# Modulation beside a feed-forward block: products on ScalarE and sums on GpSimd in place of VectorE, two steps later

## What is computed

```python
def squared_relu_mlp(h, w_up, w_down):
    return jnp.square(jax.nn.relu(h @ w_up)) @ w_down

# first block, its second half
x = x + squared_relu_mlp(rms_norm(x, norm_mlp[i]), mlp_w_up[i], mlp_w_down[i])
...
# second block: six modulation vectors for x, and for the context
mx = [m[:, None, :] for m in jnp.split(jax.nn.silu(c) @ w_mod[l] + b_mod[l], 6, axis=-1)]
mc = jnp.split(jax.nn.silu(c_ctx) @ w_mod[l] + b_mod[l], 6, axis=-1)
hx = modulate(rmsnorm(x, g_norm1[l]), mx[0], mx[1])
hc = modulate(rmsnorm(ctx, g_norm1[l]), mc[0], mc[1])
```

## Time and profile before

| | us |
|---|---|
| median of 3 runs | 3103.68 |
| lowest, highest | 3100.47, 3104.09 |
| span of the profiled execution, first to last instruction | 3102.1 |
| TensorE busy | 2953.6 |
| VectorE busy | 1820.8 |
| ScalarE busy | 1210.9 |
| GpSimd busy | 901.7 |

### The profile page before, as it was taken

One profiled execution on the slowest core, in us unless ns is written; L12 is line 12 of the kernel. 1 busy time (PEld: TensorE's weight loads), 2 busy tenths in 40 slices (PEclk: granted clock), 3 DMA queues, 4 the chain that ended last, 5 costly groups with the idle time before them and its releaser, 6 DMA issues.

```text
span 3102.1 us, 37785 instructions
## 1 busy us (share of the span) xinstructions
PE 2953.6 (95%) x14715; PEld 2445.9 (79%) x14715; DVE 1820.8 (59%) x2359; ACT 1210.9 (39%) x1929; POOL 901.7 (29%) x684
## 2 busy tenths in 40 slices
PE   7899999989999999999998999999989999999997
PEld 6688888878788888888876777888878778887886
DVE  7566566564365544333366886554574866666866
ACT  5555555553311112221334776222332444444222
POOL 5333332221000000000302886331331444443423
PEclk9999999999999999999999999999999999999999
DMA  3111111112143333111210001011023144446953
GB/s 128 41 48 48 48 48 48 42 62 102 41 129 110 111 113 102 48 48 54 93 53 21 11 9 49 28 35 35 21 75 149 40 157 150 148 148 239 371 207 122
DMA packets 96833, 274.00 MB, mean 88 GB/s; under 512 B 9232, under 2 KB 31248, under 8 KB 92176
## 3 DMA queue, kind: packets, MB, share of 16 engines
q1 hardware_dynamic: 96656, 271.58, 25.0%
HBM read 208.43 MB, written 60.36 MB: 87 GB/s over the span
## 4 chain that ended last, share of the span: by engine, by line
PE 81%; DVE 10%; ACT 4%; issue 3%; POOL 1%; DMA 1%; SPq 0%; POOLq 0%; DVEq 0%; ACTq 0%
PE ps L663 25%; PE ps L1756 11%; PE ps L3068 11%; PE ps L3729 9%; PE ps L3096 7%; DVE b L3677 2%; PE ps L2659 2%; PE ps L1060 1%; DVE b L652 1%; PE ps L2466 1%; PE ps L2437 1%; PE ps L2465 1%; PE ps L1067 1%; PE ps L2480 1%; PE ps L90 1%
## 5 line engine op out<-in xcount | busy, mean ns | idle before, releaser
L663 PE MATMUL ps<-b 128*128 128x512 f32 x3912 | 1009.6, 403 | 29.7 <-DVE b L652 14.4
L663 PEld LDWEIGHTS ps<-b 128*128 128x128 f32 x3912 | 711.4, 191 | 159.2 <-issue 20.1
L1756 PE MATMUL ps<-b 128*128 128x512 f32 x1536 | 361.7, 396 | 0.6 <-DVE b L1924 0.6
L1756 PEld LDWEIGHTS ps<-b 128*128 128x128 f32 x1536 | 288.0, 188 | 69.5 <-DVE b L1924 1.0
L3729 PE MATMUL ps<-b 128*128 128x512 f32 (+1 forms) x1464 | 326.1, 377 | 6.3 <-ACT b L3788 5.9
L3729 PEld LDWEIGHTS ps<-b 128*128 128x128 f32 x1464 | 253.8, 191 | 55.6 <-issue 10.6
L644 ACT ACTIVATE b<-b 128x1024 fp32r<-128x1024 f32 x138 | 145.2, 1054 | 319.5 <-PE ps L1756 242.3
L3121 ACT ACTIVATE b<-b 128x512 fp32r<-128x512 f32 x232 | 142.3, 615 | 270.9 <-PE ps L3096 106.3
L652 DVE TENSOR_TENSOR b<-b 128x1024 fp32r<-128x1024 f32 x138 | 174.2, 1264 | 107.6 <-ACT b L644 98.5
L3068 PE MATMUL ps<-b 128*128 128x512 f32 x960 | 225.9, 393 | 6.0 <-DVE b L3371 3.8
L3068 PEld LDWEIGHTS ps<-b 128*128 128x128 f32 x960 | 180.5, 189 | 48.3 <-DVE b L3371 7.7
(11 more groups left out here) (372 smaller groups left out, 5011.4 us busy)
## 6 DMA issues: line engine op xcount, KB each, us to landing
inner<-b SPq DMA_DIRECT2D x77, 512.0 KB, 2.6
b<-inner SPq DMA_DIRECT2D x35, 1024.0 KB, 13.5
b<-in_down SPq DMA_DIRECT2D x52, 512.0 KB, 4.3
b<-in_mod SPq DMA_DIRECT2D x96, 256.0 KB, 2.6
b<-scratch SPq DMA_DIRECT2D x46, 512.0 KB, 4.4
b<-in_gu SPq DMA_DIRECT2D x44, 512.0 KB, 4.1
b<-in_dn_in SPq DMA_DIRECT2D x32, 512.0 KB, 4.9
b<-in_up SPq DMA_DIRECT2D x32, 512.0 KB, 3.7
```

Of the source, the lines that this page charges most:

```text
L663: ins = e.matmul(ps[:, c], w, h[:, k, c], start=first and k == 0 and i == 0, stop=last and k == KT - 1 and i == 2)
L1756: ins = e.matmul(ps[:, c], w, u[:, at[k], c], start=k == 0 and p == 0, stop=k == n - 1 and p == 2)
```

## The change

The multiply-add of a weight tile is cut in two. ScalarE multiplies the loaded tile by the scalar of its partition: for k = 0 straight into `macc`, for other k into a new buffer `mprod`, one per column. GpSimd, in a new function `pool_modulation`, adds `mprod` to `macc`. ScalarE waits, before it writes `mprod` again, for the add that reads it; TensorE's small products wait for GpSimd's last add in place of VectorE's; the sync queue waits for ScalarE's product before it loads into the same buffer. All four generators pass two steps first, and the idle steps behind the twelve groups are two fewer, so that the context part's end stays where it was. The scratch for dynamic transfers is set to 1 KiB, which makes room for the new buffers.

```diff
@@ -545,6 +545,7 @@
             self.c_sq, self.c_acc = [b[:, 0:TC] for b in self.mraw], self.macc[0][:, 0:TC]
             self.m1["row"] = sb([128, T], ctx=ph)
             self.msc = sb([128, 8, 2], ctx=ph)
+            self.mprod = [sb([128, 512], ctx=ph) for _ in range(2)]
             with ExitStack() as tmp:
                 slots = [[sb([128, T], ctx=tmp) for _ in range(5)] for _ in range(2)]
             self.m1["accs"] = [s[FF1 % 5] for s in slots]
@@ -1949,13 +1950,15 @@
     def sp_modulation(self, e):
-        V = self.mm1[2]
+        A = self.mm1[1]
+        yield
+        yield
         for q in range(12):
             for k in range(KT):
                 if k >= 2:
-                    e.wait_ge(*V.at("mc", q, k - 2))
+                    e.wait_ge(*A.at("mp", q, k - 2, 1 if q < 4 else 0))
                 elif q:
-                    e.wait_ge(*V.at("mc", q - 1, k + 6))
+                    e.wait_ge(*A.at("mp", q - 1, k + 6, 1 if q <= 4 else 0))
                 e.dma_start(self.mraw[k % 2], self.a["mod"][q * KT + k]).then_inc(*self.modl[k % 2].up(q, k))
                 if k % 2:
                     yield
@@ -1965,18 +1968,20 @@
     def pe_modulation(self, e):
         P, A, V, G = self.mm1
         S = self.psl[3]
+        yield
+        yield
         for q in range(12):
             for k in range(KT):
                 if k % 2:
                     yield
-            e.wait_ge(*V.at("mc", q, KT - 1))
+            e.wait_ge(*G.at("mc", q, KT - 1, 1 if q < 4 else 0))
             if q:
                 e.wait_ge(*V.at("mt", q - 1))
             for c in range(2 if q < 4 else 1):
                 for i in range(4):
                     ins = e.matmul(blk(S, 4 * c + i), blk(self.macc[c], i), self.con("ones"), start=True, stop=True)
                 ins.then_inc(*P.up("mod", q, c))
-        for _ in range(7):
+        for _ in range(5):
             yield
         e.wait_ge(*V.at("mt", 11))
         e.wait_ge(*G.at("acc", "c", KT - 1))
@@ -1989,8 +1994,19 @@
     def act_modulation(self, e):
         P, A, V, G = self.mm1
         e.activation(self.msc.rearrange("p a b -> p (a b)"), self.par("c"), ACT.Silu).then_inc(*A.up("msc"))
+        yield
+        yield
+        e.wait_ge(*A.at("msc"))
         for q in range(12):
             for k in range(KT):
+                e.wait_ge(*self.modl[k % 2].at(q, k))
+                for c in range(2 if q < 4 else 1):
+                    if k > 1:
+                        e.wait_ge(*G.at("mc", q, k - 1, c))
+                    elif k == 0 and q:
+                        e.wait_ge(*P.at("mod", q - 1, c if q <= 4 else 0))
+                    e.activation(self.mprod[c] if k else self.macc[c], self.mraw[k % 2], ACT.Copy,
+                                 scale=self.msc[:, k, c:c + 1]).then_inc(*A.up("mp", q, k, c))
                 if k % 2:
                     yield
         e.wait_ge(*V.at("lbd"))
@@ -2002,7 +2018,7 @@
             if k >= 2:
                 e.wait_ge(*G.at("acc", "c", max(1, k - 2)))
             e.activation(self.c_sq[k % 2], self.c_x[:, k, :], ACT.Square).then_inc(*A.up("sq", "c", k))
-        for _ in range(5):
+        for _ in range(3):
             yield
         e.wait_ge(*V.at("ms", "c"))
         e.activation(self.st[:, 34:36], self.st[:, 32:34], ACT.Sqrt).then_inc(*A.up("rt", "c"))
@@ -2019,24 +2035,11 @@
     def dve_modulation(self, e):
         P, A, V, G = self.mm1
         S = self.psl[3]
-        e.wait_ge(*A.at("msc"))
+        yield
+        yield
         for q in range(12):
             n = 2 if q < 4 else 1
             for k in range(KT):
-                b = self.mraw[k % 2]
-                e.wait_ge(*self.modl[k % 2].at(q, k))
-                if k:
-                    e.wait_ge(*V.at("mc", q, k - 1))
-                elif q:
-                    e.wait_ge(*P.at("mod", q - 1, (1 if q <= 4 else 0)))
-                for c in range(n):
-                    o = self.macc[c]
-                    if k == 0:
-                        ins = e.tensor_scalar(o, b, self.msc[:, k, c:c + 1], None, ALU.mult)
-                    else:
-                        ins = e.scalar_tensor_tensor(out=o, in0=b, scalar=self.msc[:, k, c:c + 1], in1=o,
-                                                     op0=ALU.mult, op1=ALU.add)
-                ins.then_inc(*V.up("mc", q, k))
                 if k % 2:
                     yield
             for c in range(n):
@@ -2070,7 +2073,7 @@
         e.tensor_tensor(self.cw, wf, wf, ALU.mult).then_inc(*V.up())
         e.wait_ge(*V.last())
         e.tensor_scalar(self.cw, self.cw, EPS, None, ALU.add).then_inc(*V.up("cw"))
-        for _ in range(8):
+        for _ in range(6):
             yield
         st = self.st
         e.wait_ge(*P.at("cs", "c"))
@@ -2094,6 +2097,18 @@
                                        op1=ALU.subtract).then_inc(*V.up("l", "c", k - 1))
+
+    def pool_modulation(self, e):
+
+        P, A, V, G = self.mm1
+        for q in range(12):
+            for k in range(1, KT):
+                for c in range(2 if q < 4 else 1):
+                    o = self.macc[c]
+                    if k > 1:
+                        e.wait_ge(*G.at("mc", q, k - 1, c))
+                    e.wait_ge(*A.at("mp", q, k, c))
+                    e.tensor_tensor(o, o, self.mprod[c], ALU.add).then_inc(*G.up("mc", q, k, c))
     def sp_between(self, e):
         last = FF1 - 4
@@ -3545,6 +3560,7 @@
         self.pool_start(e)
         self.pool_delta(e)
         self.pool_stat(e, self.m1, self.mm1, "p")
+        self.pool_modulation(e)
         for k in range(1, KT):
             e.wait_ge(*self.mm1[1].at("sq", "c", k))
             if k > 1:
@@ -3972,7 +3988,7 @@
     from concourse.bass_utils import run_bass_kernel_spmd
     arrays = host_inputs(inputs)
-    nc = build(lambda: bacc.Bacc("TRN2", target_bir_lowering=False, num_devices=1), arrays)
+    nc = build(lambda: bacc.Bacc("TRN2", target_bir_lowering=False, num_devices=1, dynamic_dma_scratch_size=1024), arrays)
     r = run_bass_kernel_spmd(nc, [{f"in_{n}": v for n, v in arrays.items()}], core_ids=[0])
     got = r.results[0]["out"]
     return np.ascontiguousarray(got.transpose(2, 1, 0)).reshape(1, T, D)
```

## The result

The changed kernel takes 3112.31 us in the median of 9 runs (3109.27 to 3114.8); the kernel before, on the same chip, 3103.97 us. The ratio is 1.0028 with a 95% interval of 1.0019 to 1.0037, so it is slower by 0.28%, 8.3 us. The prediction said 3114.4 us, in a range from 3104 to 3119, and slower with a chance of 0.68.

The account below looks back on a forecast made before the run. TensorE, busy for 95% of the span, was taken to bound the kernel. First stall -7.5, two long waits with clock +15.4 and two short waits +2.8 gave +10.7 us: 3114.4 us, range 3104 to 3119.

Parts of the forecast that it names:

- The first stall: TensorE's 4.7 us idle before up tile 3 near 849 us, plus 2.8 us of clock, goes: -7.5 us.
- The margin that was given as 0.6 us: At the block's start, up tile 3's low half of weights would be ready 0.6 us before tile 2 ends.
- The products on ScalarE: Multiplications queued on ScalarE ahead of weight conversions and the next up tile's square and copy: 0, cover called large.
- signs of being wrong: Small products starting at once, a gap left at 849 us, or up and down tiles waiting for weights.
- The loads, the context part and the scratch: Weight loads behind ScalarE's product, context part two steps nearer its reader, smaller scratch: 0 for each.
- The add: Each of 112 adds on GpSimd takes 1.29 us, from a trace row of the same shape and type.
- The meeting with VectorE: VectorE's low half and GpSimd's add each read two tiles and hold each other up; first add begins after it.
- The waits: TensorE's small products wait for GpSimd's last add: 4.9 us twice, 1.4 us twice in the third and fourth groups.
- Rival B: Hardly any change: adds lose nothing to VectorE, waits 3.3 and about 0.7 us, +0.5 to +6.1, about 3107; chance 0.21.
- Rival C: Faster: only the first stall goes, -7.5 us, 3096; needs adds of 0.89 us without meeting VectorE; chance 0.11.
- Rival D: Worse: adds take 1.45 us or loads land late and stretch each chain, +14.5 us, 3118; chance 0.10.
- The clock behind the gaps: TensorE's lower clock after each of the two 4.9 us waits costs 2.8 us, as at the first stall.

Follow-up runs that it names:

- delay alone: The kernel before, modulation still on VectorE alone, started two steps later: 3098.22 us, ratio 0.9986.
- second pair: The changed kernel with a second pair of `macc` accumulators, TensorE's small products and VectorE's bias one step later: 3094.73 us, ratio 0.9975.
- half adds: The changed kernel with each GpSimd add on 256 of the 512 columns: 3099.62 us, ratio 0.9990.
- two engines alone: The changed kernel without the two empty steps, products on ScalarE and adds on GpSimd from step 1: 3105.67 us, ratio 1.0008.
- changed, second execution: The changed kernel run again unaltered, beside the kernel before on the same chip: 3111.44 us, ratio 1.0028.
- second pair, VectorE: The kernel before, multiply-adds on VectorE, with two accumulator pairs, small products and bias one step later, two-step delay, 1 KiB scratch: 3094.32 us, ratio 0.9971.
- asked later: The changed kernel with the small products and bias one step later, but one pair of accumulators: 3101.73 us, ratio 0.9994.

## Why the prediction held, and which terms were off

**The first stall, -7.5.** Right, and shown by the delay alone: -4.1 in the block, which is -7.5 and two new waits of 1.5. With the waits gone as well, the two versions with a second pair measure -7.7. The margin that was given as 0.6 us held: line 653's first low half starts at 847.63 and, at 1.2 us, ends near 848.8, where tile 2 ends 10.9 us after 838.57, at 849.5.

**The products on ScalarE, 0.** Right in the changed kernel. By line, as the earlier trace rows for the row it was taken from:

```profile
L2008 ACT ACTIVATE b<-b 128x512 f32<-128x512 f32 x128 | 89.7, 719 | 123.4 <-POOL b L2111 74.4 <-PE ps L1982 41.5 <-DMA b<-in_mod 7.4
```

0.719 us was measured and 0.72 predicted. The row also shows that ScalarE waits 74.4 us for the adds, one buffer per column as it is. The cover for this was called large. At the block's start it isn't: without the empty steps the products and their waits hold the weight conversions up, and the 5.51 us gap above follows. The prediction gave this queue no price and named it among the signs of being wrong.

**The loads, the context part and the scratch, 0.** Right: no new gap of TensorE names them, and the scratch alone measures 1.0001.

**The add, 1.29 us.** Right. The view of all instructions of line 2111 (minimum, median and maximum in ns):

```profile
L2111 POOL TENSOR_TENSOR b<-b x112: 1255/1300/2278, 855.3 to 1228.1; 128x512 f32<-128x512 f32 x112
...
who waited for it (us, times):
  ACT b L2008: 74.4, 65
  PEld ps L1982: 13.4, 4
  PE ps L1982: 11.7, 4
```

The median is 1.30 us; the 36 adds that meet no instruction of VectorE take 1.26 to 1.32 us, 1.29 in the mean, and all 112 take 1.38. The multiply-add that the add replaces took 0.748 us, so an add that meets nothing is 1.7 times as long. The Trainium skill, GPSIMD Engine Reference, section 4.1 (Engine selection), puts GpSimd at about 2x slower for two inputs, from which the prediction worked out an estimate of 1.50 us. The trace agrees in direction. Its 1.7 sets an add beside a multiply-add; a subtraction of two tiles of that shape takes VectorE 0.688 us in the median (line 1494 in the trace of before), and beside that the add is 1.9 times as long, near the Trainium skill's 2. For the add's own length the row of the trace was the better source.

**The meeting with VectorE.** Right as a mechanism: line 653's low half takes 1.86 us at 880.34 where its median is 1.23, and the add that starts in it takes 2.26 us where undisturbed ones take 1.29, 1.0 more. The timeline of GpSimd has that add and the two behind it:

```profile
881.09 2.26 POOL L2111 TENSOR_TENSOR b<-b 128x512 f32<-128x512 f32 x1
...
883.31 2.49 POOL L2111 TENSOR_TENSOR b<-b 128x512 f32<-128x512 f32 x2
```

The two behind it take some 1.25 us each, although VectorE's line 1941, which reads one tile from SBUF and one from PSUM, runs beside the first of them: only some of VectorE's work disturbs an add. In the kernel with half adds line 653 takes 1.24 us in the mean over the block, where it takes 1.43 in the changed kernel. The Trainium skill, SBUF — State Buffer, section "Who interferes with whom", says that a VectorE instruction with two inputs in SBUF contends with a GpSimd instruction that reads SBUF. The times of line 653 and of the add agree with it.

**The waits, 4.9 and 1.4.** Up tile 4 ends at 838.57 + 32.94 = 871.51, which is U. The eight adds last from U + 4.2 to 875.70 + 11.32 = 887.02, U + 15.5; TensorE asks at 887.08 - 4.38 = 882.70, U + 11.2, as predicted. The prediction let the adds begin at U + 4.7 and end at U + 16.2, took 4.9 of that, and 4.38 came. The short waits were 1.4 and are 1.46. Rival B, in which the adds lose nothing to VectorE, ended at U + 14.5 with a wait of 3.3: the truth lies between, nearer to the forecast. Rival C wanted adds of 0.89 us, and the half adds show what it looks like: at 0.80 us each, the time is below before's. Rival D's 1.45 us per add did not come: the mean with all meetings is 1.38.

**The clock behind the gaps, 2.8 each: the mis-sized term.** The prediction carried the 2.8 us of the first stall over to two gaps of like length. In the changed kernel the stretches behind the first gap (busy us of PE, PEld, DVE, ACT, POOL, then PEclk) read:

```profile
887.00:888.00 1.00, 0.93 (x6) 0.93 (x7) 0.00 (x0) 0.00 (x0) 0.02 (x1) 0.74 1.07 391
888.00:889.00 1.00, 1.00 (x6) 1.00 (x6) 0.15 (x1) 0.09 (x1) 0.00 (x0) 0.50 0.65 262
889.00:890.00 1.00, 1.00 (x7) 1.00 (x6) 0.01 (x1) 0.63 (x1) 0.00 (x0) 0.50 0.00 0
890.00:891.00 1.00, 1.00 (x5) 0.90 (x5) 0.16 (x1) 0.45 (x1) 0.00 (x0) 0.55 0.00 0
891.00:892.00 1.00, 1.00 (x6) 0.78 (x6) 0.00 (x0) 1.00 (x3) 0.03 (x1) 1.00 0.00 0
```

From the shares, the clock is at 0.50 (1.2 for 2.4 GHz) from 887.5 to 890.9, 3.4 us, all of it on work, and half of that is lost: 1.7 us. Behind the second gap 2.8 us of the low clock lie on work, 1.4 lost. In the kernel before the low clock went from 852.5 to 859.3, by the same view:

```profile
852.00:853.00 1.00, 0.00 (x0) 0.00 (x0) 1.00 (x2) 0.00 (x0) 0.00 (x0) 0.75 0.00 0
...
859.00:860.00 1.00, 1.00 (x5) 0.80 (x4) 1.00 (x2) 0.14 (x1) 0.00 (x0) 0.83 0.19 74
```

That is 6.8 us, of which 5.5, from 853.80 on, lie on work: the 2.8 of the prediction. So the price of that gap could not be carried over to others of about its length.

With measured terms the sum is -7.5 + 2 x 4.38 + 1.46 + 1.45 + 1.7 + 1.4 = +7.3 us, where +10.7 was predicted and the block has +8.0. Of the 3.4 us between the two sums, the clock is 2.5 and the waits 0.9. The same account, with the block's measured difference beside it (the first stall with its clock: in the kernel with the two engines alone the gap is 0.8 us longer, and the two up tiles behind it take 24.80 us where they took 24.62):

| kernel | first stall | waits for sums | clock behind them | sum | block |
|---|---|---|---|---|---|
| changed | -7.5 | 11.7 | 3.1 | +7.3 | +8.0 |
| changed, second execution | -7.5 | 11.7 | 4.0 | +8.2 | +8.9 |
| half adds | -7.5 | 1.6 | 0 | -5.9 | -5.5 |
| delay alone | -7.5 | 3.0 | 0 | -4.5 | -4.1 |
| two engines alone | +1.0 | 0.9 | 0 | +1.9 | +2.1 |
| second pair | -7.5 | 0 | 0 | -7.5 | -7.7 |
| second pair, VectorE | -7.5 | 0 | 0 | -7.5 | -7.7 |
| asked later | -7.5 | 3.5 | 2.7 | -1.3 | -1.4 |

The account closes to 0.7 us in every row. Most of what the rows with waits lack lies at the waits, which cost more than their idle time shows. TensorE's timeline in the kernel with half adds:

```profile
871.17 11.37 PE L1757 MATMUL ps<-b 128*128 128x512 f32 x48
883.34 2.05 PE L1982 MATMUL ps<-b 128*128 128x128 f32 x16 [0.80 <-POOL b L2111]
885.14 13.08 PE L1757 MATMUL ps<-b 128*128 128x512 f32 x55
```

From start to start the two down tiles take 12.17 us. Without a wait three take 889.28 - 872.48 = 16.80 us (second pair, above), so two take 11.20: the wait costs 0.97 us where the idle time reads 0.80. The sixteen small products take 1.80 us to the next start; in the kernel with the second pair they take 1.70. So this wait costs 0.27 us more than it reads, and the two of this kernel 0.5. Counted so, from the starts of the down tiles ahead of them (871.33, 971.30, 1069.20 and 1161.96), the changed kernel's four waits are 4.55, 4.55, 1.63 and 1.62 us, 12.4 in all, where the prediction had 12.6. So the clock makes nearly all of its miss in the block, 2.5 of 2.7 us.

## What to carry to other kernels

For work that runs beside a busy engine, set down for each hand-over the time at which the busy engine asks and the time at which the chain behind it ends; that difference, with the lower clock that can follow it, is the price, and it decided here between -7.7 and +8.0 us. Busy sums decided nothing: the same work on VectorE, or on ScalarE and GpSimd, gave a block of 706.3 us once TensorE no longer waited for it. Before work is moved to another engine, try to ask for its result later and to give it a second buffer; and look at what stands behind the moved work in its new queue.

## What the runs showed of the chip that was not expected

What a gap of TensorE costs in clock does not follow from its length alone. Gaps of 0.80 to 1.51 us left the clock at 1.00 in each of these traces. Of the longer ones, 5.51 us (the two engines alone) cost 3.0, 4.71 cost 2.8, two of 4.38 cost 1.7 and 1.4, and one of 3.46, in the kernel that asks later, cost 2.7: more than the two of 4.38. In the second execution of the changed kernel the first gap, again 4.38 us, was followed by this (timeline, then stretches):

```profile
889.46 3.79 PE L1982 MATMUL ps<-b 128*128 128x128 f32 x16 [4.38 <-POOL b L2111]
```

```profile
887.00:888.00 1.00, 0.00 (x0) 0.00 (x0) 0.00 (x0) 0.72 (x1) 1.00 (x1) 0.74 0.00 0
...
894.00:895.00 1.00, 1.00 (x5) 0.80 (x4) 0.00 (x0) 1.00 (x3) 0.31 (x1) 0.84 0.01 4
```

The low clock lasted from 887.5 to 894.3, 6.8 us and not 3.4, and began 2.4 us after the gap's start and not 4.8; 4.9 us of it lie on work, 2.4 lost. The same instructions after the same gap thus cost 1.7 us in one execution and 2.4 in another (the second gap 1.4 and 1.6). What decides which comes was not settled by these runs; for a forecast, 1.4 to 3.0 us for a gap of 3.5 to 5.5 us is what they bear out.
